# RMSNorm of row blocks 1 and 2 moved into the preceding sparse-attention stage, and the stick-breaking head norm done on one sum per token and head

## What is computed

```python
u = _rms_norm(h, norm1_w[layer])
proj = u @ w_in[layer]          # split into columns of group A (sparse) and B (stick-breaking)
...
o_nsa = _nsa(q_n, kc, vc, ks, vs, kw, vw, gates, ...)   # compressed, selected, window branches
o_sb = _stick_breaking(q_s, k_s, v_s)
mixed = concat([_head_rms_norm(o_nsa, nsa_out_norm_w[layer]),
                _head_rms_norm(o_sb, sb_out_norm_w[layer])])
h = h + mixed @ w_out[layer]
```

## Time and profile before

| | us |
|---|---|
| median of 3 runs | 5666.52 |
| lowest, highest | 5666.32, 6224.44 |
| the profiled execution, its own time | 5663.06 |
| its span, first to last instruction, slowest core (core 6) | 5661.5 |
| spans of the 8 cores | 5619.7 to 5661.5 |

### The profile page before, as it was taken

How to read it: one execution, slowest core, us unless ns; L and a number is a source line. 1 busy time by engine, 2 the same in 40 slices (tenths; PEclk the granted TensorE clock), 3 DMA queues, 4 the chain that set the end, 5 groups by cost and what they waited for, 6 DMA issues and landing times.

```text
span 5661.5 us, 94900 instructions; the slowest of 8 cores (5619.7 to 5661.5 us)
## 1 busy us (share of the span) xinstructions
PE 4986.2 (88%) x31936; PEld 2301.0 (41%) x31936; DVE 3136.0 (55%) x4788; ACT 3549.6 (63%) x4477; POOL 929.3 (16%) x983
## 2 busy tenths in 40 slices
PE   6888888999988878899988887889998888888998
PEld 3443332444444333244444433334444443433443
DVE  5565345757555534575755553457565645365674
ACT  3777788434367778743447788874345778786442
POOL 1000011524000001152300000115230000011431
PEclk8999899999999999999999999999999999999999
DMA  5333031855532303274542230336453313033642
GB/s 109 59 61 60 10 81 64 127 100 92 99 59 53 60 10 84 64 133 97 102 103 53 42 57 11 85 98 108 99 117 81 64 29 55 12 109 88 109 92 71
DMA packets 160710, 426.11 MB, mean 75 GB/s; under 512 B 19100, under 2 KB 19612, under 8 KB 155974
## 3 DMA queue, kind: packets, MB, share of 16 engines
q0 software_dynamic: 111456, 244.87, 27.8%
q1 hardware_dynamic: 48784, 175.17, 9.3%
HBM read 597.68 MB, written 67.11 MB: 117 GB/s over the span
## 4 chain that ended last, share of the span: by engine, by line
PE 67%; ACT 10%; DVE 9%; issue 8%; DMA 3%; POOL 1%; DVEq 0%; ACTq 0%; SPq 0%; POOLq 0%
PE ps L523 66%; ACT arena L536 10%; DVE arena L543 5%; DVE arena L552 2%; DMA arena<-w_in_r 1%; PE ps L526 1%; DVE arena L558 1%; DMA arena<-x 1%; DMA arena<-w_up_r 1%; POOL arena L543 1%; DVE arena L547 0%; DVE arena L587 0%; DVE arena L590 0%; DVE arena L1017 0%; DVEq L296 0%
## 5 line engine op out<-in xcount | busy, mean ns | idle before, releaser
L523 PE MATMUL ps<-arena 128*128 128x512 bf16 (+13 forms) x30496 | 4894.7, 320 | 581.5 <-ACT arena L536 345.0
L523 PEld LDWEIGHTS ps<-arena 128*128 128x128 bf16 (+6 forms) x30496 | 2207.1, 100 | 3213.5 <-issue 1657.6
L536 ACT ACTIVATE arena<-ps 128x1024 bf16<-128x1024 f32 (+7 forms) x2436 | 2121.6, 897 | 874.1 <-PE ps L523 812.8
L536 ACT ACTIVATE arena<-arena 128x1024 bf16<-128x1024 bf16 (+8 forms) x1472 | 1032.8, 707 | 668.7 <-DVE arena L543 502.0
L543 DVE TENSOR_TENSOR arena<-arena 128x1024 bf16<-128x1024 bf16 (+10 forms) x1264 | 773.4, 622 | 579.6 <-ACT arena L536 528.4
L552 DVE SCALAR_TENSOR_TENSOR arena<-ps,arena 128x1023 f32<-128x1023 f32 (+1 forms) x704 | 901.0, 1283 | 188.7 <-ACT arena L536 141.6
L536 ACT ACTIVATE arena<-ps,arena 128x1024 f32<-128x1024 f32 x352 | 423.6, 1205 | 529.6 <-PE ps L523 496.4
L547 DVE TENSOR_SCALAR arena<-ps 128x8 f32<-128x8 f32 (+2 forms) x460 | 250.3, 546 | 741.4 <-PE ps L523 732.7
L543 POOL TENSOR_TENSOR arena<-arena 128x1024 bf16<-128x1024 f32 (+1 forms) x224 | 519.5, 2320 | 612.2 <-DVE arena L543 388.6
L552 DVE SCALAR_TENSOR_TENSOR arena<-arena 128x2 f32<-128x2 f32 (+4 forms) x624 | 400.1, 642 | 314.9 <-ACT arena L536 277.6
L543 DVE TENSOR_TENSOR arena<-ps,arena 128x512 f32<-128x512 f32 (+2 forms) x592 | 348.2, 597 | 371.5 <-PE ps L523 355.7
(11 more groups left out here) (26 smaller groups left out, 160.8 us busy)
## 6 DMA issues: line engine op xcount, KB each, us to landing
arena<-w_up_r POOLq DMA_DIRECT2D x352, 256.0 KB, 4.5
arena<-x SPq DMA_DIRECT2D x128, 512.0 KB, 4.1
arena<-w_in_r POOLq DMA_DIRECT2D x256, 256.0 KB, 4.1
out<-arena SPq DMA_DIRECT2D x128, 512.0 KB, 3.0
arena<-w1r POOLq DMA_DIRECT2D x16, 2048.0 KB, 14.9
arena<-out SPq DMA_DIRECT2D x64, 512.0 KB, 5.1
arena<-w_down_r POOLq DMA_DIRECT2D x88, 256.0 KB, 4.8
arena<-w_tb_r POOLq DMA_DIRECT2D x16, 1024.0 KB, 8.3
```

The lines of the kernel that those rows point to most:

```text
L523: S.op('pe', lambda e, o=out, l=lhsT, rr=rhs, s0=start, s1=stop, sk=skip: e.matmul(o, lhsT=l, rhs=rr, start=s0, stop=s1, skip_group_check= ...
L536: S.op('act', lambda e, o=out, i=in_, f=func, k=kw: e.activation(out=o, in_=i, func=f, **k), r=r, w=w, cost=0.18 + 0.00084 * nel(out) + (0 ...
```

## The change

It has two parts.

**Norm.** The tiles of blocks 1 and 2 are taken out of SB0 and SB1 and made a fill of NSA0 and NSA1, between 0.2 and 0.95 of their items. They use the `x0` buffers and the ScalarE sum of squares, as block 0 does; block 3 stays in SB2 with VectorE. `uT` becomes two buffers: the old one for blocks 0, 2 and 3, and for block 1 the columns 1536 to 2047 of `mixT`, which are otherwise written only in block 3.

**Head norm.** Instead of one f32 matmul with a 128 x 128 `ones2`, four f32 matmuls take 128 tokens of `rsd` each as the stationary operand and two columns of ones as the moving one, so that the sums stand as 128 tokens by 8 (4 token tiles x 2 heads). Ln and Exp run on 128 x 8. Then eight f32 matmuls with the 8 columns, broadcast to 64 stationary columns each, and an f32 identity as moving operand lay the factors out again as 128 channels by 512 tokens in the same PSUM bank, and the last multiply reads them from PSUM.

```diff
-                if Q == 0:
+                if Q < 3:
                     xb, kx = xb0[il % 3], ('xb0', il % 3)
                     ub, ku = ub0[il % 2], ('ub0', il % 2)
...
-                    if Q <= 1:
+                    if Q < 3:
                         act(ub, xb, AF.Square, [kx], [ku, kr], accum=rc)
                     else:
                         tt('dve', xsq, xb, xb, ALU.mult, [kx], ['xsq'])
...
-                mm(psf(nb), ones2, rsd, True, True, ['ones2', 'rsd'], [('ps', nb)])
+                for tl in range(4):
+                    mm(psf(nb)[:, 2 * tl:2 * tl + 2], rsd[:, 128 * tl:128 * tl + 128], ones2, tl == 0, tl == 3, ['ones2', 'rsd'], [('ps', nb)], skip=True)
                 at(p0, 4)
-                act(rsd, psf(nb), AF.Ln, [('ps', nb), 'rsd'], ['rsd'], bias=EPS, scale=1.0 / 64)
-                act(rsd, rsd, AF.Exp, ['rsd'], ['rsd'], scale=-0.5)
-                stt('dve', mixT[...], ob, onormT[:, 4 + hp:5 + hp], rsd, ALU.mult, ALU.mult, [ko, 'onormT', 'rsd'], [('mix', Q)])
+                act(rsm, psf(nb)[:, 0:8], AF.Ln, [('ps', nb)], ['rsm'], bias=EPS, scale=1.0 / 64)
+                act(rsm, rsm, AF.Exp, ['rsm'], ['rsm'], scale=-0.5)
+                S.brk()
+                for tl in range(4):
+                    for e in range(2):
+                        mm(psf(nb)[hs[e], 128 * tl:128 * tl + 128], rsm[:, 2 * tl + e:2 * tl + e + 1].to_broadcast([128, 64]), identf, tl == 0, tl == 3, ['rsm', 'identf'], [('ps', nb)], skip=True, half=True)
+                S.brk()
+                stt('dve', mixT[...], ob, onormT[:, 4 + hp:5 + hp], psf(nb), ALU.mult, ALU.mult, [ko, 'onormT', ('ps', nb)], mixk(Q))
...
+            early = Q < 2
+            fills = [(projs_units(Q, RN, ['dve', 'act']) + projqk_units(Q, range(nh), RN, ['dve', 'act']), 0.0, 0.85)]
+            if early:
+                claim('x0')
+                fills.append((norm1_units(b, Q + 1, RN), 0.2, 0.95))
+            weave(nsa_items(Q, RN), fills, RN)
             if Q < 3:
                 claim('w1')
-                claim('x')
+                if not early:
+                    claim('x')
...
-                units += [cu[0]] + norm1_units(b, Q + 1, RS) + projn_units(Q + 1, RS, ...) + [c_1] + cu[2:]
+                units += [cu[0]] + ([] if early else norm1_units(b, Q + 1, RS)) + projn_units(Q + 1, RS, ...) + [c_1] + cu[2:]
```

More of the change, by code:

```diff
@@ L594, in build_program @@
     trix = A.alloc([128], BF16)
-    ones2 = A.alloc([128], F32)
+    identf = A.alloc([128], F32)
+    ones2 = A.alloc([2], F32)
+    rsm = A.alloc([8], F32)
     onormT = A.alloc([8], F32)
@@ L669, in init_consts @@
         ld('pool', strict, cstr_d, 'c2', 'strict')
-        ld('sp', ones2, cone_d, 'c21', 'ones2')
+        ld('sp', identf, cid_d, 'c21', 'identf')
+        for e in range(2):
+            for f in range(2):
+                memset('dve', ones2[64 * e:64 * e + 64, f:f + 1], 1.0 if e == f else 0.0, ['ones2'])
         ld('sp', onormT, onT_d, 'c22', 'onormT')
@@ L728, in build_program @@
     r1 = A.mark()
-    mixT = buf('mix', [8, 2048], BF16, [('mix', Q) for Q in R4])
+    mixT = buf('mix', [8, 2048], BF16, [('mix', Q) for Q in R4] + [('uT', 1)])
     r2 = A.mark()
-    uT = buf('att1', [8, 512], BF16, ['uT'])
+    uTs = [buf('att1', [8, 512], BF16, [('uT', 0)]), mixT[:, :, 1536:2048]]
     qa = buf('att1', [8, 512], BF16, ['qa', ('qm', 0), ('qm', 1)])
@@ L817, in build_program, with utb, utk, mixk @@
     pos = {'p': 0.0, 'z': 0, 'f': 0, 'e': 0}
+    def utb(Q):
+        return uTs[1 if Q == 1 else 0]
+    def utk(Q):
+        return ('uT', 1 if Q == 1 else 0)
+    def mixk(Q):
+        return [('mix', Q)] + ([('uT', 1)] if Q == 3 else [])
     def fbank(ring):
@@ L841, in go @@
             bk = fbank(ring)
-            chain(bk, 512, lambda dc: wch[:, dc, :], lambda dc: uT[:, dc, :], [wk, 'uT'])
+            chain(bk, 512, lambda dc: wch[:, dc, :], lambda dc: utb(Q)[:, dc, :], [wk, utk(Q)])
             eng = engs[pos['f'] % len(engs)]
@@ L874, in go @@
                     S.brk()
[L875 removed]
+                    cp('dve', utb(Q)[:, :, 128 * il:128 * il + 128], psb(bk).rearrange("p (a b) -> p a b", a=8), [('ps', bk)], [utk(Q)])
                 return go
@@ L969, in go @@
                     bk = fbank(ring)
-                    chain(bk, 512, lambda dc: uT[:, dc, 128 * il:128 * il + 128], lambda dc: wtb[:, dc, :], ['wtb', 'uT'])
+                    chain(bk, 512, lambda dc: utb(Q)[:, dc, 128 * il:128 * il + 128], lambda dc: wtb[:, dc, :], ['wtb', utk(Q)])
                     cp(engs[pos['f'] % len(engs)], vS[:, i, :], psf(bk), [('ps', bk)], [('vs', Q)])
@@ L1040, in headnorm @@
         S.brk()
-        cp('act', mixT[:, 2 * g:2 * g + 2, 512 * Q:512 * Q + 512], psb(bk).rearrange("p (a b) -> p a b", a=2), [('ps', bk)], [('mix', Q)])
+        cp('act', mixT[:, 2 * g:2 * g + 2, 512 * Q:512 * Q + 512], psb(bk).rearrange("p (a b) -> p a b", a=2), [('ps', bk)], mixk(Q))
     def at(p0, lag):
@@ L1173, in go @@
                 nb = fbank(ring)
-                mm(psf(nb), ones2, rsd, True, True, ['ones2', 'rsd'], [('ps', nb)])
+                for tl in range(4):
+                    mm(psf(nb)[:, 2 * tl:2 * tl + 2], rsd[:, 128 * tl:128 * tl + 128], ones2, tl == 0, tl == 3, ['ones2', 'rsd'], [('ps', nb)], skip=True)
                 at(p0, 4)
-                act(rsd, psf(nb), AF.Ln, [('ps', nb), 'rsd'], ['rsd'], bias=EPS, scale=1.0 / 64)
-                act(rsd, rsd, AF.Exp, ['rsd'], ['rsd'], scale=-0.5)
-                stt('dve', mixT[:, 4 + hp, 512 * Q:512 * Q + 512], ob, onormT[:, 4 + hp:5 + hp], rsd, ALU.mult, ALU.mult, [ko, 'onormT', 'rsd'], [('mix', Q)])
+                act(rsm, psf(nb)[:, 0:8], AF.Ln, [('ps', nb)], ['rsm'], bias=EPS, scale=1.0 / 64)
+                act(rsm, rsm, AF.Exp, ['rsm'], ['rsm'], scale=-0.5)
+                S.brk()
+                for tl in range(4):
+                    for e in range(2):
+                        mm(psf(nb)[hs[e], 128 * tl:128 * tl + 128], rsm[:, 2 * tl + e:2 * tl + e + 1].to_broadcast([128, 64]), identf, tl == 0, tl == 3, ['rsm', 'identf'], [('ps', nb)], skip=True, half=True)
+                S.brk()
+                stt('dve', mixT[:, 4 + hp, 512 * Q:512 * Q + 512], ob, onormT[:, 4 + hp:5 + hp], psf(nb), ALU.mult, ALU.mult, [ko, 'onormT', ('ps', nb)], mixk(Q))
         return go
@@ L1377, in c_1 @@
                     cu[1]()
-                units += [cu[0]] + norm1_units(b, Q + 1, RS) + projn_units(Q + 1, RS, ['act', 'dve'] if Q == 0 else ['dve']) + [c_1] + cu[2:]
+                units += [cu[0]] + ([] if early else norm1_units(b, Q + 1, RS)) + projn_units(Q + 1, RS, ['act', 'dve'] if Q == 0 else ['dve']) + [c_1] + cu[2:]
             else:
```

8 lines of the change are left out of this document (2 added, 6 removed).

## The result

| | before | changed |
|---|---|---|
| comparable executions, us | 5666.32 to 5667.51 | 5693.91, 5693.94, 5700.31 |
| ratio, first measurement | 1 | 1.0052 [1.0029, 1.0074] |
| ratio, second measurement, same kernel | 1 | 1.0091 [1.0053, 1.0130] |

A forecast was written before the change was run, and what follows sets the result against it. No attention stage has a full engine, PE and ACT passing work back and forth; the MLP is TensorE alone. Stage terms sum to -14 us a sequence, -56 over four, from 5666.5 to 5610 us; range 5540 to 5675.

The forecast's parts named there:

- NSA0 +3, SB0 -8: Per sequence, NSA0 3 us longer from block 1's norm; SB0 8 us shorter without it, head norm included.
- NSA1 +2: NSA1 takes block 2's norm and grows 2 us a sequence, as busy shares leave room but queues are in order.
- SB1 -7: SB1 loses block 2's norm and gets 7 us shorter a sequence, head norm included, with DVE falling to 52 us.
- Head norm, 2.5 us of PE, 0.42 of ACT: Each new head norm, sixteen a sequence, takes 2.5 us of PE, 1.2 more than before, and 0.42 of ACT.
- SB2 -2, SB3 -2, nothing behind them: Head norm makes SB2 and SB3 each 2 us shorter a sequence, ACT being slightly fuller; later stages get nothing.
- NSA3, counted at nothing: The stage NSA3 was given no term in the sum: a change of 0 us a sequence.
- rival 2: A wait on `w_in_r` loads or the `x0` claim replaces the removed one in SB0 and SB1: 5665 us, chance 0.23.
- The claim of `x0`: SB0 and SB1 might wait at their start until the fourth tile frees the `x0` buffers; the forecast counted nothing.
- Rival 3: TensorE's f32 head-norm passes take 4.5 us and decide, from about 3.4 if all on the path: 5705 us, chance 0.12.
- the two signs of being wrong: PE's f32 work over 3.4 us a head pair, or NSA0 growing by more than SB0 shrinks.

The follow-up runs named there:

- e2: The kernel before with the head norm change alone, norm stages as before: mean core span 5695 us against 5647, ratio 1.0101.
- e1: The kernel before with the norm move of blocks 1 and 2 alone, old head norm: mean core span 5645 us against 5647, ratio 1.0012.
- e14: e1 with each moved tile's eight transposes written four times, planned order kept: mean core span 5679 us, ratio to before 1.0062.
- e16: e6 with block 2's sum of squares on VectorE instead of ScalarE, in NSA1: mean core span 5591 us, no ratio.
- e3: The changed kernel as it is, run again: mean core span 5684 us against 5647 before, ratio 1.0091.
- e6: The changed kernel with the head norm's squares, ones, factors and identity in bf16, same order: mean core span 5573 us, ratio to before 0.9862.
- e7: The kernel before with the norm move for block 1 alone, old head norm: mean core span 5644 us, ratio 0.9991.
- e8: The kernel before with the planner told the true f32 matmul cost, same instructions in another order: mean core span 5638 us, no ratio.
- e11: The kernel before with its one head-norm matmul in bf16, TensorE order unchanged: mean core span 5623 us, ratio 0.9956.
- e13: e1 with the old form of the head norm in bf16, order as in e1: mean core span 5621 us, ratio to before 0.9940.
- e4: The changed kernel with the planner told the true f32 matmul cost, same instructions in another order: mean core span 5650 us, ratio to before 1.0002.
- e9: The bf16 head norm in its new form with the norm move for block 1 alone: mean core span 5572 us, ratio to before 0.9874.
- e10: e6 with two unused 128x512 f32 ScalarE operations added to each head norm: mean core span 5623 us, no ratio.
- e12: e2 with the new head norm in bf16, TensorE order as in e2: mean core span 5603 us, ratio to before 0.9889.
- e5: e4 with eight unused bf16 matmuls of 512 columns before each head norm's sums: mean core span 5688 us, ratio to before 1.0058.

## Why the prediction was wrong, by its steps

**NSA0 +3, SB0 -8: right**, +4.1 and -7.1, with some luck: the -8 contained the head norm, which adds 6.9 us to SB0 by itself (e2) and takes 1.6 off it with the norm moved (changed against e1). In e1 SB0 lost 19 us of ACT and 11.5 of PE over four sequences and 21.9 us of time. The mechanism was as told: no `x` in the chain, `w_in_r` issued early, DVE of SB0 at 25.7.

**NSA1 +2: mis-sized**, +5.3, and +6.0 with the norm alone. I let the busy shares say that there was room. Transposes in these stages are paid at 0.85 (e14), and more on DVE costs too (e16). The clock is not the reason: half-clock time in NSA1 over four sequences is 16 us before and 17 in the changed kernel. In e1 it is 39.

**SB1 -7: mis-sized**, -4.4 with the norm alone, -0.9 in all. DVE fell to 53 as forecast and ACT to 78, and the stage did not follow: its half-clock time rose from 41 to 63 us in e1, and with the head norm (after against e1) it is 3.5 us a sequence longer again. PE's new waits for `w_in_r` in SB1 account for 1.4 us a sequence.

**Head norm, 2.5 us of PE, 0.42 of ACT: right** to 0.1 us. By the Trainium skill (TensorE: Matmul & The Clock Gate, "LDWEIGHTS") the loads alone were estimated at 1.7 us. Where PE runs free at 2.4 GHz (core 0 of e3), two-column passes start 0.112 us apart and pairs of 64-column passes 0.109, together 8 x 0.112 + 8 x 0.109 = 1.8 us, which agrees. At 1.2 GHz both are 0.213 apart, as a fifth of the first and over a third of the second are. The rest of the 2.6 us busy I have not split further.

**SB2 -2, SB3 -2, nothing behind them: this step failed.** It is the step that turns the head norm's work into time. The prediction had +6 for PE and -4 for ACT in proportion, and took -2, as "ACT is the slightly fuller one, and the new PE work is independent of the items". So PE's 80 us were priced at next to nothing. The head norm alone costs 46 us in the stage table (e2, cores 0 to 3), and taking its PE work down by 120 us in the same order takes 111 us off the kernel (e6). SB2 came to +0.1 and SB3 to +1.1, both inside the bounds of -4 to +2; the larger part lies where nothing was counted, NSA3 +3.4 and behind SB3 +3.4. ACT's share was indeed the higher, but a busy share doesn't price an engine: at 0.79 for PE and 0.36 for ACT the same quantities give a loss. The PE queue is in order, so passes that depend on nothing of the next item still stand before it; and the planner had room of 0.56 us for them.

**Where the 25 us a sequence between -14 and +11 lie:** SB1 6.1, NSA3 3.4, behind SB3 3.4, NSA1 3.3, SB3 3.1, SB2 2.1, NSA2 1.4, NSA0 1.1, SB0 0.9.

**NSA3, counted at nothing: +3.4.** The head norm of the last pair of SB2 falls into its start. The first 24 us there, before (core 0) and then after (core 0), columns as in the earlier trace rows:

```profile
2026.00:2034.00 8.00, 5.37 (x34) 2.54 (x33) 2.78 (x4) 5.05 (x6) 0.53 (x1) 1.00 0.15 15
2034.00:2042.00 8.00, 4.86 (x65) 3.22 (x64) 0.75 (x1) 5.43 (x7) 0.00 (x0) 1.00 0.57 116
2042.00:2050.00 8.00, 7.69 (x88) 4.85 (x89) 1.92 (x8) 5.89 (x7) 0.00 (x0) 1.00 0.01 2
```

```profile
2056.20:2064.00 7.80, 5.29 (x37) 2.91 (x37) 2.77 (x4) 4.83 (x5) 0.53 (x1) 1.00 0.17 19
2064.00:2072.00 8.00, 5.87 (x46) 4.12 (x47) 0.75 (x1) 1.41 (x3) 0.00 (x0) 0.55 0.56 115
2072.00:2080.00 8.00, 6.95 (x59) 4.61 (x59) 0.69 (x4) 4.22 (x5) 0.00 (x0) 0.59 0.01 2
2080.00:2090.00 10.00, 9.40 (x103) 5.88 (x102) 2.68 (x10) 7.32 (x8) 0.00 (x0) 1.00 0.00 0
```

Before, the clock stays at 1.00 and 88 matmuls pass in the third window; after, it falls to 0.55 and 0.59 and 59 pass. The f32 sums, from 2063.3 us, stand just before the fall. But e6, with the head norm in bf16, has a clock of 0.59 in its window there as well, so f32 doesn't decide it:

```profile
2024.00:2032.00 8.00, 5.40 (x52) 3.49 (x48) 0.75 (x1) 2.96 (x3) 0.00 (x0) 0.59 0.54 113
```

Half-clock time in NSA3, over four sequences, is 17 to 34 us in the profiles with the old form (before, e1, e7, e8, e11, e13), f32 or bf16, and 37 to 51 with the new form (e2, e3, e4, e6, e9, e10, e12, e16), f32 or bf16, in five different orders. In e5, where eight dense matmuls stand before the sums, it is 22. So the fall goes with the new form, two visits of short passes, and dense work in front of them takes most of it away. In the changed kernel it adds 24 us of half-clock time, which at 0.31 is some 7 of the 14 us that NSA3 grew.

**The rivals.** Of rival 2 a part came. Its sign, a `w_in_r` load of over 8 us in the chain, is there in SB1 (9.98), but PE waits only 1.4 us a sequence more for it; over the span these waits are 24 us, no single one above 5.1. The claim of `x0` held nothing up: in SB0 and in the first 15 us of SB1 (sequence 2, core 6) ScalarE waits for PE and for nothing else. Rival 3 named the right engine with the wrong point: it let TensorE decide from 3.4 us a head pair, and 2.59 were enough. The threshold was counted from a gain of 14 us a sequence, of which 11 were those of SB1, SB2 and SB3, and the 1.2 us already in the sum were charged far below 0.79. The time is near its 5705 by luck, since that stood for 4.5 us a head pair. Neither of the two signs of being wrong came: PE's f32 work stayed under 3.4 us, and NSA0 grew by less than SB0 shrank. The signs looked at quantities, and it was the prices that were wrong. The range ended at 5675 because the forecast and rival 2 shared the low price of PE.

**A faster kernel.** In bf16 the new head norm pays: e6 and e9 beat both kernels, with 0.9862 and 0.9874, at the price of rounding the squares and the factors. The old form in bf16 gives 0.9956 and 0.9940. Between the forms (e12 against e11, e6 against e13) are 20 and 49 us; 28 and 34 are what the clock accounts for, with half-clock time at 411 and 392 against 502 and 501. Without it the new form is 8 us slower in the first pair and 15 faster in the second.

## What to carry to other kernels

Price moved or added work by engine, not by busy share: where two engines pass work back and forth, take some row or run that shows what a microsecond on each is worth, and do not call work on an in-order queue hidden because nothing depends on it. Look also at the stage behind the one that gets the work: half of the loss lay there. Before an operation of a new kind enters a planned order, give the planner its true cost, and time the control too; here another order was worth 26 to 34 us to the changed kernel and 8 to 9 to the one before, so a difference of that size between two planned kernels may be the order's. When TensorE's work is made sparser, read the granted clock with it: a saving in work may be returned by the clock.
